# mLSTM values and the recurrence's inner values as seven block products with tokens stationary; a layer's forget rows by column groups

## The reference

```
seg = split((x @ w_in) + b_in)          # q, k, v, o, gates | q, f, i, g | merge gates
mLSTM:  v = x @ W_v + b_v               # 512 tokens (latent, context) x 1024 columns
HGRN2:  i = x @ W_i + b_i               # 512 tokens (latent in column order, context) x 1024 columns
        S_t = diag(f_t) S_{t-1} + k_t i_t^T ;  o_t = S_t^T q_t   (both directions)
```

## Time and profile before

| | us |
|---|---|
| median of 3 runs | 1975.35 (1972.21 to 1975.98) |
| profiled execution, its own time | 1971.99 |
| its span in the trace | 1970.2 |
| PE busy | 1945.2 (99%) |
| DVE, ACT, POOL busy | 1241.7, 565.9, 218.7 |

### The profile page before, as it was taken

The page is one execution under the profiler, slowest core; times in us unless marked ns, Lnnn a source line. Parts: engine busy times, 40 slices in busy tenths (PEclk is TensorE's granted clock), DMA queues, the critical chain, the costliest instruction groups (busy, mean ns, idle before and its releaser), DMA issues.

```text
span 1970.2 us, 31165 instructions
## 1 busy us (share of the span) xinstructions
PE 1945.2 (99%) x12449; PEld 1751.1 (89%) x12449; DVE 1241.7 (63%) x2513; ACT 565.9 (29%) x1363; POOL 218.7 (11%) x267
## 2 busy tenths in 40 slices
PE   9999999999999999999999999999999999999998
PEld 7878999977799998888888888888888989999998
DVE  5425897572378865899669565343456765766664
ACT  3343332224533313111110013322343323132212
POOL 6100430312014200000000001001212100000000
PEclk9999999999999999999999999999999999999999
DMA  6354555343545542555545364332222224545552
GB/s 199 112 187 137 165 165 161 111 151 114 172 150 171 182 140 79 182 166 164 166 152 173 116 190 136 119 90 86 86 65 67 83 67 148 172 134 167 171 177 81
DMA packets 272105, 273.60 MB, mean 139 GB/s; under 512 B 7982, under 2 KB 269338, under 8 KB 271962
## 3 DMA queue, kind: packets, MB, share of 16 engines
q1 hardware_dynamic: 270152, 267.65, 42.5%
q0 software_dynamic: 1216, 3.32, 0.6%
q10 hardware_dynamic: 594, 0.65, 0.1%
HBM read 270.38 MB, written 1.08 MB: 138 GB/s over the span
## 4 chain that ended last, share of the span: by engine, by line
PE 93%; DVE 4%; ACT 1%; issue 1%; DMA 1%; ACTq 0%; DVEq 0%; SPq 0%; PEldq 0%
PE bank L818 50%; PE bank L1324 10%; PE bank L796 8%; PE bank L1510 5%; PE bank L1559 2%; PE bank L966 2%; PE bank L1087 1%; PE bank L1610 1%; PE bank L1037 1%; PE bank L1494 1%; PE bank L1572 1%; PE bank L1046 1%; PE bank L1391 1%; PE bank L1235 1%; PE bank L1241 1%
## 5 line engine op out<-in xcount | busy, mean ns | idle before, releaser
L818 PE MATMUL bank<-arena,SQ 128*128 128x136 f32 (+2 forms) x2176 | 341.4, 308 | 0.1
L818 PEld LDWEIGHTS bank<-arena,SQ 128*128 128x128 f32 x2176 | 307.0, 191 | 17.2 <-ACT arena L1931 0.3
L818 PE MATMUL bank<-arena,W 128*128 128x136 f32 (+2 forms) x1824 | 272.6, 301 | 2.7 <-issue 2.1
L818 PEld LDWEIGHTS bank<-arena,W 128*128 128x128 f32 x1824 | 247.6, 191 | 15.4 <-issue 4.1
L1931 ACT ACTIVATE H<-bank 128x128 f32<-128x128 f32 (+1 forms) x260 | 82.3, 317 | 535.5 <-PE bank L818 535.5
L818 PE MATMUL bank<-U,W 128*128 128x136 f32 (+2 forms) x1296 | 194.6, 303 | 0.0
L818 PEld LDWEIGHTS bank<-U,W 128*128 128x128 f32 x1296 | 176.4, 191 | 11.0 <-issue 2.9
L796 PE MATMUL bank<-U,W 128*128 128x272 f32 (+1 forms) x576 | 133.1, 392 | 1.4 <-ACT U L2213 0.8
L3033 DVE SCALAR_TENSOR_TENSOR W<-W,CC 128x256 f32<-128x256 f32 x280 | 128.3, 483 | 7.0
L796 PEld LDWEIGHTS bank<-U,W 128*128 128x128 f32 x576 | 109.0, 190 | 24.6 <-issue 2.3
L818 PE MATMUL bank<-arena 128*128 128x136 f32 (+1 forms) x1024 | 124.1, 278 | 0.0
(11 more groups left out here) (459 smaller groups left out, 3117.9 us busy)
## 6 DMA issues: line engine op xcount, KB each, us to landing
W<-in_ffn_w_up_dram SPq DMA_DIRECT2D x44, 1024.0 KB, 5.1
W<-in_ffn_w_in_dram SPq DMA_DIRECT2D x44, 1024.0 KB, 5.1
W<-in_ada_w_dram SPq DMA_DIRECT2D x36, 1024.0 KB, 6.6
W<-in_mix_w_in_dram SPq DMA_DIRECT2D x36, 1024.0 KB, 5.3
W<-in_ffn_w_down_dram SPq DMA_DIRECT2D x16, 1408.0 KB, 6.6
W<-in_ffn_w_out_dram SPq DMA_DIRECT2D x16, 1408.0 KB, 6.3
W<-in_w_in_dram SPq DMA_DIRECT2D x21, 1024.0 KB, 5.3
W<-in_w_out_dram SPq DMA_DIRECT2D x8, 1024.0 KB, 8.5
```

The source lines that it names most:

```text
L818: last = mm(o, a(k), b[:, k], start=not adds and k == 0, stop=k == kt - 1, skip_group_check=True)
```

## The change

`project_values` and `steps_i` become seven products with tokens stationary: seven products of 4 k steps x 2 token tiles, each matmul with 128 moving columns, 56 matmuls in place of 32. A step of `steps_i` is now two matmuls of 128 columns, and there are 28 of them; `ctx` in `WEAVE` goes from 12 to 8, the other counts stay. POOL makes the four weight sums for each of these strips as well, and in the mLSTM stage three of the four token sums (DVE the first). ACT makes four more copies a strip. DVE joins them. In the recurrence DVE's two bias additions are replaced by `inner_late` after level 1 and `inner_rest` after level 2, and POOL adds the bias to all of `HI` in one operation of 128x1024. DVE's `token_sums(permuted_and_context, TBR)` in the second mLSTM pair goes; POOL makes them after the last pair. In the layers, the forget rows are computed in four groups of 32 columns and folded by a second matmul, and the first query tile goes into bank 5 ahead of them.

```diff
@@ TensorE, layers
-                forget_rows()
-                for r in (0, 1, 2, 3):
+                first_query_tile()        # bank 5, waits for each piece of us
+                forget_parts()
+                second_query_tile()       # bank 1
+                forget_fold()
+                for r in (1, 2, 3):
                     slot_fm(r, u1, T1)
...
+            def forget_parts():
+                eng.wait_ge(S.land[3], p.next(S.land[3], 16))
+                take(4)
+                for kk in range(KD):
+                    g = 32 * (kk % 4)
+                    last = mm(bank[4][g:g + 32, 0:T1], W[3][:, kk, 0:32], u1(kk), start=kk < 4, stop=kk >= 4, skip_group_check=True)
+                last.then_inc(S.done[3], p.inc(S.done[3]))
+            def forget_fold():
+                take(4)
+                mm(bank[4][0:HEADS, 0:T1], SEL[:, 0:HEADS], FT, start=True, stop=True).then_inc(S.gf_full, p.inc(S.gf_full))
@@ TensorE, steps_i (project_values has the same products and waits)
+                eng.wait_ge(S.land[r], p.next(S.land[r], 16))
+                take(2)
+                for k in range(4):
+                    ins = add(2, near, permuted_and_context(0, 0), raw(0, 0), k, True)      # two matmuls of 128 columns
...
+                take(3)
+                eng.wait_ge(S.wsum, p.next(S.wsum))
+                    ins = add(3, near, TBR[0], WSR[0], k, True)
...
+                eng.wait_ge(S.snap, p.next(S.snap))
+                    add(2, far, permuted_and_context(1, 0), raw(0, 1), k, False)
...
+                eng.wait_ge(S.snap, p.next(S.snap))
+                    ins = add(3, far, TBR[3], raw(1, 1), k, False)
...
+                    ins = add(2, near, TBR[1], WSR[1], k, False)
...
+                    ins = add(3, near, permuted_and_context(1, 1), WSR[3], k, False)
...
+                eng.wait_ge(S.wsum, p.next(S.wsum))
+                eng.wait_ge(S.snap, p.next(S.snap))
+                    ins = add(2, near, TBR[2], WSR[2], k, False)
@@ ScalarE, recurrence
+            def kept_inner(which):
+                x, z, y = bank[2][:, 0:SEQ], bank[3][:, 0:SEQ], bank[3][:, SEQ:2 * SEQ]
+                for n in which:
+                    eng.wait_ge(S.prod, p.next(S.prod, 2 if n == 2 else 1))
+                    i, src = ((0, x), (3, z), (1, x), (2, y))[n]
+                    act(SNI[i], src, ACT.Copy).then_inc(S.snap, p.inc(S.snap))
...
+                kept_inner((0,))
                 lookup(i, 0)
+                kept_inner((1,))
...
                 for lev in range(2, 7):
                     eng.wait_ge(S.lev_full, p.next(S.lev_full))
                     lookup(i, lev)
-                    if more and lev == 2:
+                    if lev == 2:
+                        kept_inner((2, 3))
+                    if more and lev == 3:
                         kept(0, (0,))
-                    if more and lev == 3:
+                    if more and lev == 4:
                         kept(0, (1,))
-                    if more and lev == 4:
-                        kept(0, (2,))
                     if more and lev == 5:
-                        kept(0, (3,))
+                        kept(0, (2, 3))
+                    if lev == 6:
+                        eng.wait_ge(S.hi, p.next(S.hi))
+                        p.skip(S.hi)
+                    if more and lev == 6:
                         kept(1, (0,))
@@ VectorE, recurrence
                     if lev == 1:
-                        inner(i, 0)
-                    if lev == 3:
-                        inner(i, 1)
+                        inner_late()              # waits for 4 copies; one 256-wide add, frees bank 3
+                    if lev == 2:
+                        inner_rest()              # waits for 6 products; a 256-wide and a 512-wide add, frees bank 2
@@ GpSimd, recurrence
+            for i in range(PAIRS):
+                strip_sums(3)
+                if i + 1 < PAIRS:
+                    strip_sums(0)
+                inner_bias(i)                     # waits for hi; HI += bias, 128x1024
+                if i + 1 < PAIRS:
+                    strip_sums(1)
```

More of the change, by code:

```diff
@@ L801, in u1, with first_query_tile, second_query_tile @@
                 return U[:, kk, 0:T1]
-            def forget_rows():
+            def first_query_tile():
+                eng.wait_ge(S.land[0], p.next(S.land[0], 16))
+                take(5)
+                for kk in range(KD):
+                    eng.wait_ge(S.us, p.now(S.us) - (KD - 1 - kk))
+                    last = mm(bank[5][:, 0:T1], W[0][:, kk, 0:P], u1(kk), start=kk == 0, stop=kk == KD - 1)
+                last.then_inc(S.half[0], p.inc(S.half[0]))
+            def second_query_tile():
+                take(1)
+                for kk in range(KD):
+                    last = mm(bank[1][:, 0:T1], W[0][:, kk, P:2 * P], u1(kk), start=kk == 0, stop=kk == KD - 1)
+                last.then_inc(S.done[0], p.inc(S.done[0]))
+            def forget_parts():
                 eng.wait_ge(S.land[3], p.next(S.land[3], 16))
@@ L1472, in _ @@
             p.leave("memory")
+            places["sums"] = (p.now(S.prod), p.now(S.wsum), p.now(S.tsum))
             project(first=True)
[L1474 removed]
+            project_values(True)
             gate_columns()
@@ L1552, in steps_i @@
             def steps_i(r):
-                eng.wait_ge(S.land[r], p.next(S.land[r], 16))
[L1555 to L1563, removed]
+                near, far = 0, SEQ
@@ new lines, in raw, with add @@
+                def raw(t, h):
+                    return W[r][:, 4 * h:4 * h + 4, t * P:(t + 1) * P]
+                def add(b, c, tok, w, k, clear):
+                    for n in range(2):
+                        last = mm(bank[b][:, c + n * P:c + (n + 1) * P], tok[:, k, n * P:(n + 1) * P], w[:, k],
+                                  start=clear and k == n == 0, stop=k == 3, skip_group_check=True)
+                    return last
+                eng.wait_ge(S.land[r], p.next(S.land[r], 16))
@@ new lines, in steps_i @@
+                take(2)
+                for k in range(4):
+                    ins = add(2, near, permuted_and_context(0, 0), raw(0, 0), k, True)
+                    if k == 3:
+                        ins.then_inc(S.prod, p.inc(S.prod))
+                    yield
+                take(3)
+                eng.wait_ge(S.wsum, p.next(S.wsum))
+                for k in range(4):
+                    ins = add(3, near, TBR[0], WSR[0], k, True)
+                    if k == 3:
+                        ins.then_inc(S.prod, p.inc(S.prod))
+                    yield
@@ L1565, in steps_g @@
+                eng.wait_ge(S.wsum, p.next(S.wsum))
+                eng.wait_ge(S.snap, p.next(S.snap))
+                for k in range(4):
+                    ins = add(2, near, TBR[2], WSR[2], k, False)
+                    if k == 0:
+                        ins.then_inc(S.done[r], p.inc(S.done[r]))
+                    if k == 3:
+                        ins.then_inc(S.prod, p.inc(S.prod))
+                    yield
+                p.skip(S.snap)
             def steps_g(r):
@@ L1639, in _ @@
             p.leave("recurrence")
-            places["sums"] = (p.now(S.prod), p.now(S.wsum))
             queries = steps_q(2)
@@ L2395, in kept @@
                         p.skip(S.done[d])
+            def kept_inner(which):
+                x, z, y = bank[2][:, 0:SEQ], bank[3][:, 0:SEQ], bank[3][:, SEQ:2 * SEQ]
+                for n in which:
+                    eng.wait_ge(S.prod, p.next(S.prod, 2 if n == 2 else 1))
+                    i, src = ((0, x), (3, z), (1, x), (2, y))[n]
+                    act(SNI[i], src, ACT.Copy).then_inc(S.snap, p.inc(S.snap))
+                    if n == 3:
+                        p.skip(S.prod)
             def forget(i, d, t):
```

188 lines of the change are left out of this document (149 added, 39 removed).

## The result

The changed kernel takes 2032.11 us (median of 4 runs, 2031.63 to 2033.79), the kernel before 1973.78 in the same session: ratio 1.0301, 95% interval 1.0288 to 1.0313. The profiled span is 2030.3 us against 1970.2, so 60.1 us longer. The direction was forecast; 2006 and the range up to 2024 were too low.

A forecast was written before the change was run, and what follows sets the result against it. TensorE, busy for 99% of the span, was taken to bound the kernel. Savings of 15.3 us, new waits of 38.4 and a clock loss of 11 gave +34.1, hence 2006 us, range 1980 to 2024.

The forecast's parts named there:

- savings, with the bank 5 wait: TensorE's shorter matmul work in mLSTM strips, recurrence and layers saves 15.3 us, less a 1.4 wait in the first layer.
- first mLSTM pair: ScalarE's copy 1 stands behind the gate exponentials, so TensorE waits 0.3 us, between 0 and 3.
- waits in three pairs: New TensorE waits in three recurrence pairs, 5.0, 0.4 and 6.1 us in each.
- last pair: In the last recurrence pair only the wait before the seventh inner product exists, 2.2 us.
- clock in the recurrence: TensorE's clock falls in long pauses; five of seven waits lose 2.2 us each: 11 us, bounds 0 and 15.
- factor of 1.45: Skill's slower pace for weight load and matmul pairs; would lose some 34 us over eight strips; given no weight.
- Wait a: TensorE before the seventh inner-value product, for ScalarE's copy 2 behind a lookup: 5.0 us, bounds 4.4 and 6.4.
- Wait b: TensorE before the third product of the next forget strip, for copy 0 behind a lookup: 0.4 us.
- Wait c: TensorE before the next forget strip's fourth product, for copy 1 behind a lookup: 6.1 us, bounds 5.1 and 7.3.
- rival 3: All the waits come but TensorE's clock stays up: 1995 us, chance 0.15.
- Rival 4: GpSimd's sums and wide addition hold VectorE in every pair and all seven clock prices are paid: 2018 us, chance 0.11.

The follow-up runs named there:

- the layers alone: Kernel before the change with only the layers' part added (forget rows in four column groups and a fold, first query tile in bank 5): 1969.86 us.
- first experiment: Changed kernel with ScalarE's copies 2 and 3 of the inner values moved ahead of the lookup behind level 2: 2009.43 us.
- the bias away: Changed kernel with GpSimd's inner bias moved behind the four weight sums of strip 1: 2032.62 us.
- all corrections: Changed kernel with inner and forget copies earlier on ScalarE, GpSimd's bias behind strip 1's sums, four first-strip mLSTM copies ahead of the gate exponentials: 1981.99 us.
- the bias behind the last pick: Against the kernel with all corrections: forget copies behind the lookups of levels 2 to 5, GpSimd's bias after the pair's last pick: 1973.82 us.
- The two orders: Changed kernel with inner copies 2 and 3 ahead of level 2's lookup and forget copies 0 and 1 behind lookups 2 and 3: together 1998.94 us.

## Why the prediction was wrong, point by point

Against the steps of the sum (+34.1 forecast, 60.1 measured in the profiled spans):

| step | forecast | measured |
|---|---|---|
| savings, with the bank 5 wait | -13.9 | -12.6 |
| first mLSTM pair | 0.3 | 9.9 |
| waits in three pairs | 34.5 | 40.8 |
| last pair | 2.2 | 4.4 |
| clock in the recurrence | 11 | 13.9 |
| not attributed one by one | | 3.7 |

- The savings: right in pace. 48 passes take 5.36 from start to start, 0.1117 each, as forecast from the earlier trace rows; a later mLSTM strip takes 12.60. The factor of 1.45 that the prediction worked out from the Trainium skill ("TensorE: Matmul & The Clock Gate", Back-to-back issue gap) and gave no weight is not there. The layers gave 2.1 in this trace for 3.1 forecast (3.0 in the trace of the layers alone); the wait for bank 5 was 1.25 for 1.4.
- Wait a: right in place and size, 5.1 for 5.0. TensorE asked 3.1 us behind level 0 (1415.30 to 1418.4), as forecast. The first experiment shows the cause.
- Wait b: 0.4 forecast, none, since wait a had held TensorE back and ScalarE's copy was there in time. It showed once wait a was gone (1.8 in the first experiment).
- Wait c: right in place, too small: 8.15 for 6.1, above the upper bound of 7.3. The bound charged one GpSimd operation, priced from the earlier trace rows. There are two in a row, and each holds VectorE to its end: 4.45 - 1.30 = 3.15 on top of the 5.1 without a neighbour gives 8.25. With the bias away the wait measured 5.3, so the 5.1 was right.
- The last pair: 1.8 of 2.2 at a, and 2.6 that I did not have, before level 4, by the same bias (the scans take 3.47 for 1.30).
- **The step that failed** is the pricing of GpSimd beside VectorE: "0.3, between 0 and 3 (two of POOL's operations of 1.46 holding VectorE's gate chain up)". Seven operations of 1.5 to 3.1 us stand beside that chain. Four gate scans alone went from 2.55 to 8.64, and the two rows of 40x512 gained 0.7 each (1.37 and 1.43 for 0.68 and 0.69). The strip lost 9.9 against its 12.5: a wait of 7.35 and the slow passes behind it. This is 9.6 of the 26 us that are missing, and with wait c (6.2) and the last pair (2.2) the neighbour accounts for 18, the slow passes of the first strip counted in. That GpSimd's operations are what lengthens VectorE's is shown by a run for the carry (4.45 to 1.30 when the bias is away). For the gate chain it rests on rows: the scans take 2.56 in the run with the layers alone, which has no sums there, but also none of the other mLSTM work, and no run took the sums alone away. The delay of the chain makes a wait only because copy 1 stands behind the exponentials, which the prediction saw: with the copies ahead of them the scans still take 8.64, and the strip takes 12.6.
- The clock: the mechanism was right, rival 3 is out. The size was 14 in the recurrence for 11: TensorE's busy time of a pair, 64.98 against 60.92 in the run with all corrections, which has the same work and the clock up, is 4.1 a pair, and 1.7 in the last (51.46 against 49.76 in the run with the bias behind the last pick). The price of 2.2 was taken from the start of the program; behind wait a it was about 3 and behind c about 1.6. The first mLSTM strip pays a further 2.3 that stand in its 9.9.
- Rival 4 (a longer chain by GpSimd, 2018, chance 0.11) had the mechanism. It charged 2.6 a pair and nothing in the mLSTM stage.
- The 3.7 not attributed: about 3.1 are in the three pairs. At full clock TensorE is busy for 60.92 of such a pair and was for 61.19, so 0.3 less where the pace gives 1.3; the rest goes into stalls of 0.1 to 0.2 and the last pass ahead of each wait. A wait behind the recurrence went from 1.0 to 1.7.

## What to carry to other kernels

When work is given to an idle engine, list what the engine beside it does in the same microseconds. GpSimd at 14% looked free, but its operations here held VectorE's scans and sums for up to their full length, and the bias cost wherever GpSimd ran it: moving it within GpSimd moved the wait, and moving it to VectorE removed it. A copy that TensorE waits for belongs ahead of any instruction in its engine's queue that waits for a longer chain. Read the waits again after each correction, because one wait hides the next: wait b showed only when wait a was gone, and VectorE's only when wait c was gone. The two orders gave 22.7 and 9.1 us apart and 33 together; with the mLSTM copies, the last forget copies and the bias put right too it was 62.

## What the runs showed of the hardware

- Scans of VectorE of 128x255 take 0.65 alone and 2.85 with a GpSimd operation of 2.34 beside them; gate scans of 8x256 go from 0.64 to 2.16, so the cost follows GpSimd's length and not VectorE's size. An operation of 128x512 with a scalar operand goes from 0.55 to 1.49 beside GpSimd's sums.
- GpSimd is lengthened too: a sum of 128x512 takes 1.27 with VectorE idle and 3.11 at 1184.88, beside two constants and a sum of 128x1024 of VectorE; which of them lengthens it is not shown.
- In a pause the clock fell 4.3 us behind the last matmul at wait a, 4.4 at wait c and 5.2 in the first mLSTM strip, and 2.65 behind the end of the kernel before. It stayed at half for 6.1 us of work after wait a, 4.7 after the mLSTM wait and about 3.1 after wait c (1443.70 to 1446.8). So one price for a pause does not hold.
